# An order of keys, queries, values in a convolution stage, an eighth weight buffer for the experts, and semaphores cleared beside them

## What is computed

```python
# gated delta rule branch, per head of 128
qkv_g = silu(centred_depthwise_conv(qkv_g, conv_w[l]))      # 5 taps along the tokens
qg, kg, vg = split(qkv_g)                                   # 8 heads each
qg = l2norm(qg); kg = l2norm(kg)                            # the values are not normed
o_fwd, o_bwd = gated_delta_rule_chunked(...)                # the next stage
...
x = x + merged @ w_out
# experts: each of the 16 experts takes its 64 best tokens of 512
h2 = rmsnorm(x, norm2_w)
x = x + expert_choice_ffn(h2, w_router, w_gate, w_up, w_down)   # 1024 -> 2048 -> 1024
return rmsnorm(x, norm_f_w)
```

## Time and profile before

| | us |
|---|---|
| median of 3 runs | 2566.94 (2565.26 to 2567.37) |
| the profiled execution | 2568.99, of it 2567.2 span |
| TensorE busy | 2307.6 (90%) |
| VectorE busy | 880.3 (34%) |
| ScalarE busy | 540.9 (21%) |
| GpSimd busy | 165.2 (6%) |
| DMA | 488.52 MB, mean 190 GB/s |

### The profile page before, as it was taken

One profiled execution on the slowest core, in us unless ns is written; L12 is line 12 of the kernel. 1 busy time (PEld: TensorE's weight loads), 2 busy tenths in 40 slices (PEclk: granted clock), 3 DMA queues, 4 the chain that ended last, 5 costly groups with the idle time before them and its releaser, 6 DMA issues. The chain is left out here.

```text
span 2567.2 us, 30502 instructions
## 1 busy us (share of the span) xinstructions
PE 2307.6 (90%) x12724; PEld 1180.9 (46%) x12724; DVE 880.3 (34%) x1550; ACT 540.9 (21%) x959; POOL 165.2 (6%) x166
## 2 busy tenths in 40 slices
PE   6999999979999989997998888989898877999877
PEld 3444554447777764453333333333333223574343
DVE  1215766645766731113011010101010114444672
ACT  2004656632322313010000000000000003223131
POOL 0000000023433310000000000000000000120000
PEclk9999999989999999998999999999999998999889
DMA  5211000010111015235999999999999982202010
GB/s 196 72 58 68 34 34 1 0 42 27 26 35 27 26 59 197 113 125 214 427 428 428 428 427 428 428 428 428 427 427 428 428 345 68 67 33 70 33 49 34
DMA packets 93404, 488.52 MB, mean 190 GB/s; under 512 B 10781, under 2 KB 37683, under 8 KB 68563
## 3 DMA queue, kind: packets, MB, share of 16 engines
q1 hardware_dynamic: 91920, 486.34, 46.6%
q10 hardware_dynamic: 1347, 0.22, 0.0%
HBM read 483.14 MB, written 3.41 MB: 190 GB/s over the span
## 5 line engine op out<-in xcount | busy, mean ns | idle before, releaser
L1467 PE MATMUL PS<-SL,R 128*64 128x512 f32 x1168 | 262.3, 598 | 40.0 <-DMA SL<-w_gate 20.5
L1467 PE MATMUL PS<-R 128*64 128x512 f32 x880 | 197.3, 596 | 27.1 <-DMA R<-w_up 15.2
L1467 PEld LDWEIGHTS PS<-SL,R 128*64 128x64 f32 x1168 | 81.2, 137 | 216.2 <-issue 146.4
L1919 PE MATMUL PS<-HT,SL 128*128 128x512 f32 x384 | 169.6, 597 | 2.2 <-PEq L1662 2.2
L1635 DVE TENSOR_TENSOR HT<-HT,PS 128x512 f32<-128x512 f32 x32 | 20.6, 684 | 367.8 <-PE PS L1467 367.8
L1487 PE MATMUL PS<-SL,HT 128*64 128x512 f32 x280 | 124.4, 594 | 14.9 <-ACT HT L1575 7.0
L1467 PEld LDWEIGHTS PS<-R 128*64 128x64 f32 x880 | 60.8, 137 | 158.3 <-issue 108.7
L1488 PE MATMUL PS<-SL,HT 128*64 128x512 f32 x280 | 124.9, 596 | 0.0
L630 PE MATMUL PS<-HT,SL 128*128 128x512 f32 x256 | 119.2, 620 | 0.8 <-PEq L420 0.8
L348 PE MATMUL PS<-HT,SL 128*128 128x512 f32 x256 | 115.7, 606 | 3.5 <-PEq L235 2.6
L1640 DVE COPY HT<-PS 64x512 f32<-64x512 f32 x16 | 10.9, 684 | 305.5 <-PE PS L1488 305.5
(11 more groups left out here) (371 smaller groups left out, 3585.9 us busy)
## 6 DMA issues: line engine op xcount, KB each, us to landing
SL<-w_up SPq DMA_DIRECT2D x38, 2048.0 KB, 28.0
SL<-w_gate SPq DMA_DIRECT2D x35, 2048.0 KB, 30.2
SL<-w_down SPq DMA_DIRECT2D x35, 2048.0 KB, 27.3
R<-w_gate SPq DMA_DIRECT2D x29, 2048.0 KB, 29.5
R<-w_down SPq DMA_DIRECT2D x29, 2048.0 KB, 27.2
R<-w_up SPq DMA_DIRECT2D x26, 2048.0 KB, 29.2
SL<-w_in SPq DMA_DIRECT2D x19, 2048.0 KB, 8.8
X<-w_in SPq DMA_DIRECT2D x16, 512.0 KB, 3.9
```

What stands on the lines that cost most here:

```text
L1467: m = pe.matmul(banks[n][half * CAP:(half + 1) * CAP, :], XC[x // 2 % 2][:, 2 * j + k, toks], w[:, k, (2 * half + n) * 512:(2 * half + n + ...
L1919: m = pe.matmul(bank_[:, :], slab(i % 2)[:, k, j * P:(j + 1) * P], hT[:, k, :], start=(k == 0), stop=(k == KD - 1))
```

## The change

Three things are changed.

1. In the convolution stage the order in a head is key, query, value. TensorE's list is written out anew, with a projection ahead of each `sums`; ScalarE keeps the Silu table over a key and the query behind it; VectorE multiplies a unit (L754 before) two units later instead of one.
2. The ring has an eighth buffer, R[6]. `Sel` has two small buffers, and VectorE makes one pair's selection while the pair before it is worked on. The first pair's gather goes in two halves between the first slabs of the first expert.
3. The two blocks that clear semaphores are gone. GpSimd clears 71 semaphores of earlier stages inside the stage with the experts, where it has nothing else to do.

```diff
-        def clear_spent():
-            with nc.Block() as block:
-                @block.gpsimd
-                def _(pool):
-                    for s_ in spent:
-                        pool.sem_clear(s_)
+        def clear_spent(pool):
             for s_ in spent:
+                pool.sem_clear(s_)
                 counts.pop(id(s_), None)
...
-        SEQ = [u for i in range(HEADS) for u in (i, HEADS + i, 2 * HEADS + i)]
+        SEQ = [u for i in range(HEADS) for u in (HEADS + i, i, 2 * HEADS + i)]
...
+                project(0)
+                for i in range(HEADS):
+                    k, q, v = SEQ[3 * i:3 * i + 3]
+                    project(2 * i + 1)
+                    sums(k)
...
+                    if i + 1 < HEADS:
+                        project(2 * i + 2)
+                    sums(q)
+                    turn(k)
+                    turn(v)
...
-                for p in range(NC3 + 3):
-                    if 1 <= p <= NC3 and SEQ[p - 1] in NTH:
+                for p, u in enumerate(SEQ):
+                    if p % 3 != 1:
+                        nc.scalar.preload_act_table(ACT.Silu)
+                    act.wait_ge(conv_done, p + 1)
+                    a(cp(conv[p % 3], conv[p % 3], ACT.Silu), silu_done)
...
+                    if p % 3 == 1:
                         norm(SEQ[p - 1])
+                    elif p % 3 == 2:
+                        norm(SEQ[p - 1])
+                        evac_turned(SEQ[p - 2])
+                        evac_turned(u)
...
-                    if 1 <= p and SEQ[p - 1] in NTH:
-                        u = SEQ[p - 1]
+                    if 2 <= p and SEQ[p - 2] in NTH:
+                        u = SEQ[p - 2]
...
-        Sel = R[6][:, :].rearrange("p (t n) -> p t n", t=NT)
+        Sel = [R[4][:, 2048 + i * 512:2560 + i * 512].rearrange("p (t n) -> p t n", t=NT) for i in range(2)]
...
-        RING = [R[1], R[2], R[3], SL[3], SL[2], SL[0], SL[1]]
+        RING = [R[1], R[2], R[3], SL[3], SL[2], SL[0], SL[1], R[6]]
...
+            @block.gpsimd
+            def _(pool):
+                clear_spent(pool)
...
+                        if x == 0 and part == 0 and j % 2 == 0:
+                            gather(0, j // 2)
+                            pe.wait_ge(E7["xc"], j // 2 + 1)
...
+                select(0)
+                select(1)
                 for q in range(NPAIR):
-                    v(tt(sel_of(q), iota.unsqueeze(1).unsqueeze(1).to_broadcast([P, NT, 2, CAP]), of_pair(posm3, q), ALU.is_equal), E6["sel"])
-                for q in range(NPAIR):
+                    if 1 <= q < NPAIR - 1:
+                        dve.wait_ge(E7["xg"], 2 * q)
+                        select(q + 1)
...
-        spent.extend([p5, gate5, merge5, m5, out5, *E4.values(), *E6.values(), *E7.values()])
-        clear_spent()
```

More of the change, by code:

```diff
@@ L655, in turn @@
                     m.then_inc(tr3, 1)
-                for p in range(NC3 + 2):
-                    if 1 <= p <= NC3 and SEQ[p - 1] in NTH:
-                        sums(SEQ[p - 1])
-                    if p == 2:
+                project(0)
[3 more added lines that the diff above has]
+                    sums(k)
+                    if i == 0:
                         pe.wait_ge(pre["g_ready"], 1)
@@ L696, in _ @@
                 a(cp(v16(beta), ab3[:, :, 16:32], ACT.Exp, scale=-1.0), pre["sp_ready"])
-                for p in range(NC3 + 3):
-                    if 1 <= p <= NC3 and SEQ[p - 1] in NTH:
-                        norm(SEQ[p - 1])
[L700 to L709, removed]
+                for p, u in enumerate(SEQ):
[3 more added lines that the diff above has]
+                    a(cp(conv[p % 3], conv[p % 3], ACT.Silu), silu_done)
+                    if u in NTH:
+                        n = NTH[u]
+                        if n >= 2:
+                            act.wait_ge(qk_norm, n - 1)
+                        a(cp(sq[n % 2], conv[p % 3], ACT.Square), sq3)
+                    if p % 3 == 1:
+                        norm(SEQ[p - 1])
+                    elif p % 3 == 2:
+                        norm(SEQ[p - 1])
+                        evac_turned(SEQ[p - 2])
+                        evac_turned(u)
+                    if p == 1:
                         act.wait_ge(pre["G_ready"], 1)
@@ L713, in _ @@
                         a(cp(decs, decs, ACT.Exp), pre["sp_ready"])
-                    if p >= 5 and p % 3 == 2:
-                        evac_turned(SEQ[p - 4])
-                        evac_turned(SEQ[p - 3])
             @block.vector
@@ L753, in _ @@
                         dst = gq[:, u, :] if u < HEADS else gk[:, u - HEADS, :]
-                        v(tt(dst, conv[(p - 1) % 3], sq[n % 2], ALU.mult), qk_norm)
+                        v(tt(dst, conv[(p - 2) % 3], sq[n % 2], ALU.mult), qk_norm)
                     if p == 0:
@@ L1329, in expert_slab @@
             eng.dma_start(RING[r % NR][:, :], src).then_inc(ring_in[r % NR], 16)
+        spent.extend([proj_done, raw_ready, rot_done, rope_done, slab_used, va_evac, score_done, max_ready,
+                      exp_done, pd_ready, pT_done, pT_ready, pv_done, oT_evac, rstd2, sq_ready, ss_done, norm_done,
+                      cf_done, cf_evac, wab_in, ab_done, ab_evac, p3_done, conv_done, silu_done, sq3, ss3, rstd3, qk_norm,
+                      tr3, tr3_evac, *pre.values(),
+                      *[E4[n] for n in E4 if n not in ("sq4", "ss4", "rstd4", "og_ready")]])
         with nc.Block() as block:
@@ L1449, in gather @@
                             m = pe.matmul(OB[hf][:, c * P:(c + 1) * P], h2[:, t, 256 * j + k:256 * (j + 1):2],
-                                          Sel[:, t, q * P:(q + 1) * P], start=(t == 0), stop=(t == NT - 1))
+                                          Sel[q % 2][:, t, :], start=(t == 0), stop=(t == NT - 1))
                     m.then_inc(E7["xg"], 1)
@@ L1489, in down @@
                     m.then_inc(E7["used"], 1)
-                gather(0, 0)
-                gather(0, 1)
                 for q in range(NPAIR):
-                    pe.wait_ge(E7["xc"], 2 * q + 2)
+                    if q:
+                        pe.wait_ge(E7["xc"], 2 * q + 2)
                     for e in range(2):
```

9 lines of the change are left out of this document (3 added, 6 removed).

## The result

The changed kernel takes 2527.59 us (median of 4 runs, 2526.58 to 2527.88), the kernel before in the same session 2567.15 us (2565.26 to 2570.39). The ratio is 0.9844, with a 95% interval of 0.9827 to 0.9861, and the difference of the medians is 39.6 us. 2526 was predicted, 40.8 less than before. The profiled execution took 2527.79 us, of it 2525.6 span, which is 41.6 less than before.

A forecast was written before the change was run, and what follows sets the result against it. Experts were taken as bound by the slab stream, the convolution stage by TensorE, which still waits. Gains of 25.2 + 8.4 + 0.3 + 6.9 = 40.8 us from the median 2566.94 gave 2526 us, range 2520 to 2535.

The forecast's parts named there:

- The convolution stage: Convolution stage: TensorE no longer waits, a head takes 16.33 us instead of 20.30; gain 25.2 us, bounds 16 and 27.
- The clears: Two block ends that cleared semaphores: gaps of 3.71 and 5.47 us fall to 0.41; gain 8.4 us, bounds 6 and 9.
- The shorter standstill: Before merge and router: TensorE stands still some 2 us instead of 5.2, saving 0.3 us at 1.2 GHz.
- Buffer and split gather: Start of the experts: slab stream gains 4.9 us by buffer, 3.8 by split, less a 1.8 pause; 6.9 us together.
- The hole of 1.8 us: First expert: slab stream pauses 1.8 us before slab 10, behind the second half of the gather.
- Selection per pair, reload at the end: Experts: VectorE's selection near 0.7 us a pair and the later reloads of SL[0] and SL[1] cost nothing.
- the rival of a slower stream: Expert stream: eighth buffer slows every slab by 0.22 us, to 5.12 us or 410 GB/s, cancelling the gain; chance 0.02.
- ScalarE as the pace: Convolution stage: table switches cost twice their row, a head loses 1.0 us of its gain, 2534 us; chance 0.10.

The follow-up runs named there:

- clears twice: The kernel before with each semaphore cleared twice, 108 more clears on the way: 2576.82 us against 2568.57, ratio 1.0033.
- the run with four more loads: The changed kernel with two more table loads ahead of each norm, four a head, 32 in all: 2548.08 us, 20.5 above the changed kernel's median.

## Why the prediction was right

- **The convolution stage** (25.2 predicted, 25.3 measured, 25.0 alone). The head was a count of rows at 2.4 GHz, 16.33 us, and it came out at that. Laid out from the last value projection, the end was forecast 10.0 us long (499.9 to 509.9) and was 10.0 (497.43 to 507.45). All of it lay 2.3 us earlier by the clock of unchanged stages ahead. What was off had no part in the sum: the 3.97 us lost per head were lost in six heads, in the seventh only the wait. How close 25.2 and 25.3 are is luck of the trace. Four more traces have the old list of this stage without an edit (clears alone, buffer, split, clears twice): there 7, 6, 4 and 6 of the seven waits were followed by the low clock, and the stage took 167.4, 165.5, 163.6 and 166.0 us, with 166.2 before. The new list took 140.8 to 141.0 us in all five traces in which it stands as it is. So the stage gives 22.6 to 26.6 us, depending on which execution of the old list it is compared with.
- **The clears** (8.4 predicted and measured, alone too). The price of a single clear was not right: 0.055 us from the difference of the two gaps, 0.071 to 0.075 by the doubled clears. The sum didn't rest on it, since it took the gaps whole. 71 of them are 5.3 us on GpSimd, and a second 5.3 were hidden as well.
- **The shorter standstill** (0.3 predicted, 0.2 measured) was mis-sized, and the 0.2 is luck. Where the next stage follows the gap of 3.7 or 6.4 us, its first 10 us ran at a mean clock of 0.69 to 0.84; behind a gap of 0.48 us they ran at 1.00 in five traces and at 0.83 in three, that of the changed kernel among these. Merge and router took 209.5 to 211.3 us in the six traces with the gap and 207.7 to 209.4 in the eight without, 1.8 less in the mean, which can be why the median with the clears alone fell by 9.3 us and not by the 8.4 of the gaps. Windows of the kernel before and of the run with the clears alone:

```profile
962.87:972.87 10.00, 9.95 (x19) 4.41 (x20) 0.00 (x0) 6.33 (x9) 0.00 (x0) 0.79 0.92 326
...
959.55:969.55 10.00, 9.94 (x23) 4.48 (x24) 0.50 (x1) 8.14 (x12) 0.00 (x0) 1.00 0.93 325
```

- **Buffer and split gather** (6.9 predicted and measured). Alone they give 4.9 from the first issue on and 2.2 from the gather on, against 4.9 and 2.0. The hole of 1.8 us is 1.7 in the windows and disappears when the gather is moved back.
- **Selection per pair, reload at the end**: nothing, as said. VectorE is busy 88 of 820 us in the stream and the stream stays at 428 GB/s, which also ends the rival of a slower stream.
- **ScalarE as the pace** did not come about, but its step was mis-sized. The prediction took the slack as TensorE's time less ScalarE's busy time, 16.33 - 12.2 = 4.1 us, left out 1.1 us that the list itself waits and loses between instructions, and priced four more loads at 8 us, since it counted only steady heads, by 1.0 each. Measured: a slack of 3.0, 2.1 a head in six heads, and 10.1 us at the stage's start and end, 22.8 in all beside the 1.0 of the first projections. In the timeline of the last head, an activation ends at 503.43 and the load behind it starts at 503.45, the load ends at 504.73 and the next activation starts at 504.75; the loads put in cost 1.28 us each. The Trainium skill, page "ScalarE: Activation LUTs", section "What ACT_TABLE_LOAD costs", adds a drain of about 1380 ns to every switch; by that four switches would put ScalarE's chain at 13.3 + 5.5 = 18.8 us and the head with it, an estimate. The head of the changed kernel took 16.33 us, and the rows show the 1283 ns and no drain on either side of a load.

One thing stays open: why the clock in the unchanged stages ahead differs between executions. It moved the convolution stage's start between 364.5 and 369.3 us. By the medians the kernel gained 39.6, by the profiled executions 41.2; the difference of 1.6 is of that size.

## What to carry to other kernels

Where one engine is full and still waits, add up its work per round from rows at the full clock: that sum is what a better order of the other engines' lists can reach, and the clock comes back with it. The slack of an engine in a round is the round less its whole chain with the waits inside it, not less its busy time, and what is hidden in the middle of a loop is bare at its start and end. Where the low clock follows some waits and not others, the stage differs between executions, and its gain is read over several traces. Housekeeping between two stages, such as clearing semaphores, is paid in full at a barrier and is free on an engine that has nothing to do in the next stage.

## What the runs showed of the hardware

- A wait of 1.90 to 2.03 us on TensorE was followed by a stretch at 1.2 GHz in six of seven heads of the kernel before (eight turned matmuls in 1.48 to 1.91 us instead of 1.04), and once not; over five traces of this list in 29 of 35. Waits of 1.67 us in the run with four more loads left the window of the head at 1.00.
- 1.88 us of useless matmuls in place of such a wait made a head 1.67 us shorter.
- A semaphore clear on GpSimd takes 0.071 to 0.075 us; a block end without clears 0.3 to 0.5 us.
- The same 32 matmuls at the start of the convolution stage took between 15.55 and 16.54 us in the eight traces with the new list. In the window from 371 to 373 us the granted clock was 1.00 in the changed kernel (stage from 367.02, 15.55 us) and 0.52 in the run with four more loads (from 367.73, 16.54 us).
